# Expert weights in 4 MB transfers with rows of 32 KB into four double slots, in place of 2 MB transfers into eight slots

## What is computed

```
def expert_choice_ffn(h, w_router, w_gate, w_up, w_down):
    probs = softmax(einsum('bld,de->ble', h, w_router))     # 16 experts
    gate, idx = lax.top_k(transpose(probs, (0, 2, 1)), cap) # cap = 2 * 512 / 16 = 64 tokens an expert
    xs = h[idx]                                             # 16 x 64 x 1024
    a = einsum('becd,edf->becf', xs, w_gate)                # f = 2048
    u = einsum('becd,edf->becf', xs, w_up)
    y = einsum('becf,efd->becd', silu(a) * u, w_down)
    y = y * gate[..., None]
    return segment_sum(y, idx)                              # added back to the 512 tokens
```

## Time and profile before

| | us |
|---|---|
| median of 3 runs | 1852.03 (1851.35 to 1852.34) |
| the profiled execution | 1852.32 |
| its span in the trace | 1850.5 |
| TensorE matmuls busy in it | 1714.0 (93%) |
| weight loads of TensorE | 1045.3 |
| DVE busy | 658.1 |
| ACT busy | 447.3 |
| the queue of SP, share of 16 DMA engines | 66.0% |

### The profile page before, as it was taken

How to read it: one execution, slowest core, us unless ns; L and a number is a source line. 1 busy time by engine, 2 the same in 40 slices (tenths; PEclk the granted TensorE clock), 3 DMA queues, 4 the chain that set the end, 5 groups by cost and what they waited for, 6 DMA issues and landing times. The chain is left out here.

```text
span 1850.5 us, 20537 instructions
## 1 busy us (share of the span) xinstructions
PE 1714.0 (93%) x8653; PEld 1045.3 (56%) x8653; DVE 658.1 (36%) x916; ACT 447.3 (24%) x561; POOL 0.2 (0%) x4
## 2 busy tenths in 40 slices
PE   7999996999897997979979889799999999999998
PEld 6888873343332432324324243277778888888886
DVE  8985633001010110100101001057645565645745
ACT  5434331110000100101001010065333433423333
POOL 0000000000000000000000000000000000000000
PEclk9999998999999999999999999999999999999999
DMA  6235437999999999999999999970422223222311
GB/s 201 93 113 178 161 135 288 409 429 427 427 429 427 430 429 427 429 429 428 429 427 429 429 427 429 427 273 17 160 68 71 89 91 114 91 91 91 114 46 46
DMA packets 75050, 492.55 MB, mean 266 GB/s; under 512 B 7408, under 2 KB 11504, under 8 KB 49904
## 3 DMA queue, kind: packets, MB, share of 16 engines
q1 hardware_dynamic: 74992, 491.71, 66.0%
HBM read 487.49 MB, written 2.10 MB: 265 GB/s over the span
## 5 line engine op out<-in xcount | busy, mean ns | idle before, releaser
L1244 PE MATMUL ps<-xs,xe 128*64 128x512 f32 x2048 | 461.5, 598 | 67.2 <-DMA xs<-w_up 34.7
L1244 PEld LDWEIGHTS ps<-xs,xe 128*64 128x64 f32 x2048 | 141.8, 137 | 379.5 <-issue 264.5
L1256 PE MATMUL ps<-xs,hidT 128*64 128x512 f32 x960 | 215.0, 596 | 10.7 <-DMA xs<-w_down 6.6
L422 DVE TENSOR_TENSOR lo<-raw,hi 128x2048 fp32r<-128x2048 f32 x72 | 162.7, 2260 | 150.3 <-ACT hi L413 147.1
L1509 DVE TENSOR_TENSOR hid<-hid,ps 128x512 f32<-128x512 f32 x32 | 20.6, 684 | 525.8 <-PE ps L1244 525.8
L413 ACT ACTIVATE hi<-raw 128x2048 fp32r<-128x2048 f32 x72 | 136.1, 1890 | 185.0 <-PE ps L452 93.9
L476 PE MATMUL ps<-xh,hi 128*128 128x512 f32 x416 | 165.2, 397 | 2.3 <-issue 1.3
L476 PE MATMUL ps<-xl,hi 128*128 128x512 f32 x416 | 162.4, 390 | 0.0
L452 PE MATMUL ps<-xh,hi 128*128 128x512 f32 x384 | 150.2, 391 | 1.4 <-DVE xt L2088 1.1
L452 PE MATMUL ps<-xl,hi 128*128 128x512 f32 x384 | 149.5, 389 | 0.0
L1256 PEld LDWEIGHTS ps<-xs,hidT 128*64 128x64 f32 x960 | 68.8, 137 | 135.9 <-issue 112.7
(11 more groups left out here) (442 smaller groups left out, 1783.9 us busy)
## 6 DMA issues: line engine op xcount, KB each, us to landing
xs<-w_up SPq DMA_DIRECT2D x64, 2048.0 KB, 32.8
xs<-w_gate SPq DMA_DIRECT2D x64, 2048.0 KB, 32.0
xs<-w_down SPq DMA_DIRECT2D x60, 2048.0 KB, 31.1
raw<-w_in SPq DMA_DIRECT2D x24, 1024.0 KB, 7.8
raw<-ffn_up_w SPq DMA_DIRECT2D x24, 1024.0 KB, 5.1
raw<-ffn_down_w SPq DMA_DIRECT2D x12, 1024.0 KB, 5.0
raw<-w_out SPq DMA_DIRECT2D x8, 1024.0 KB, 5.1
xs<-w_down_q SPq DMA_DIRECT2D x2, 2048.0 KB, 36.7
```

The costliest lines, as they stand in the source:

```text
L422: dve.tensor_tensor(lo[slot][:, 0:size], raw[:, raw_slot(n), 0:size], hi[slot][:, 0:size].bitcast(F32), ALU.subtract).then_inc(sem("lo_don ...
L1244: mm = pe.matmul(ps[64 * half:64 * half + 64, bank + b, :], xe[:, k, CAP * u:CAP * (u + 1)], xs[n % NXS][:, f:f + 512], start=(k == 0), st ...
L1256: mm = pe.matmul(ps[64 * nn:64 * nn + 64, YB, :], hidT[:, 4 * (c % 2) + kk, CAP * half:CAP * (half + 1)], xs[n % NXS][:, kk * D + nn * 512 ...
```

## The change

Two chunks become one transfer of 4 MB. `expert_rows` gives 512 rows of w_gate or w_up, four to a partition, or 1024 rows of w_down, eight to a partition, 32 KB in one piece. Slots are four double tiles `xd`, and the old slots `xs` are halves of them, at places of their own. The first sixteen chunks are still issued as halves (`load_half`: 16 KB of each partition's 32 KB), each when the chunk eight before it is used; from chunk 16 on `load_x` issues a double transfer when both chunks of its slot are used. TensorE waits at even chunks only, for both halves or for the double transfer. The gather now takes every fourth column, the transposes every eighth, and they begin only when both halves of hid are made. The last four quarters stay as they are, with semaphores of their own (`q_sem`).

```diff
+NXD = NXS // 2
...
-    small[:, P_GX:NPRM] = i["norm2_g"][0].reshape(4, P, 2).transpose(1, 0, 2).reshape(P, KD)
+    small[:, P_GX:NPRM] = i["norm2_g"][0].reshape(2, P, 4).transpose(1, 0, 2).reshape(P, KD)
...
-        xs = [at(f"xs{j}", [P, XCH], F32, (0, 16, 32, 48, 102, 118, 64, 80)[j]) for j in range(NXS)]
+        xd = [at(f"xd{j}", [P, 2 * XCH], F32, (0, 32, 102, 64)[j]) for j in range(NXD)]
+        xs = [xd[j // 2][:, XCH * (j % 2):XCH * (j % 2) + XCH] for j in range(NXS)]
...
-        def expert_chunk(n, i=None):
-
-            e, j = divmod(n, 12)
+        def expert_rows(m, i=None):
+
+            e, j = divmod(m, 6)
             first = e if i is None else i * 2 + e
-            if j < 8:
-                return (wg, wu)[j // 4][bass.ds(first * D + 256 * (j % 4), 256), :].rearrange("(p k) n -> p (k n)", k=2)
-            return wd[bass.ds(first * FF + 512 * (j - 8), 512), :].rearrange("(p k) n -> p (k n)", k=4)
+            if j < 4:
+                return (wg, wu)[j // 2][bass.ds(first * D + 512 * (j % 2), 512), :].rearrange("(p k) n -> p k n", k=4)
+            return wd[bass.ds(first * FF + 1024 * (j - 4), 1024), :].rearrange("(p k) n -> p k n", k=8)
...
         def x_arrived(pe, n, i):
 
-            slot = n % NXS
-            before = 16 * in_first[2 * slot] if slot < 2 else 16 * (slot >= 5)
-            pe.wait_ge(x_sem(slot), i * (16 * 24 // NXS) + (before + 16 * (n // NXS + 1)))
+            base = 16 if n % NXS >= 6 else 0
+            if n % 2 == 0:
+                pe.wait_ge(x_sem(n), base + 32 if isinstance(i, int) and i == 0 and n < NXS else i * (16 * 24 // NXS) + (base + 48 + 16 * (n // NXS)))
...
         def gather(pe, k):
 
             o = ps[:, TB + k // 2 % 2, (k % 2) * P:(k % 2 + 1) * P]
-            d0 = 256 * (k // 2) + k % 2
+            d0 = 512 * (k // 4) + k % 4
             for t in range(NT):
-                mm = pe.matmul(o, htk[:, t, d0:d0 + 255:2], s1[:, t, :], start=(t == 0), stop=(t == NT - 1))
+                mm = pe.matmul(o, htk[:, t, d0:d0 + 509:4], s1[:, t, :], start=(t == 0), stop=(t == NT - 1))
...
+                    pe.wait_ge(sem("hid_done"), i * 4 + (2 * u + 2))
                     for b in range(2):
-                        pe.wait_ge(sem("hid_done"), i * 4 + (2 * u + b + 1))
                         for q in range(4):
-                            f = 512 * b + q
-                            mm = pe.transpose(ps[:, TB + b, q * P:(q + 1) * P], hid[:, f:f + 509:4], ident)
+                            f = 4 * b + q
+                            mm = pe.transpose(ps[:, TB + b, q * P:(q + 1) * P], hid[:, f:f + 1017:8], ident)
...
-            def load_x(n, i=None):
-
-                if i is not None:
-                    sp.wait_ge(sem("xs_used"), i * 24 + (n - NXS + 1))
-                elif n >= NXS:
+            def load_half(n):
+
+                if n >= NXS:
                     sp.wait_ge(sem("xs_used"), n - NXS + 1)
-                sp.dma_start(xs[n % NXS][:], expert_chunk(n, i)).then_inc(x_sem(n % NXS), 16)
+                rows = expert_rows(n // 2)
+                k = rows.shape[1] // 2
+                d(xs[n % NXS].rearrange("p (k n) -> p k n", k=k), rows[:, k * (n % 2):k * (n % 2) + k, :]) \
+                    .then_inc(x_sem(n), 16)
+
+            def load_x(m, i=0):
+
+                sp.wait_ge(sem("xs_used"), i * 24 + (2 * (m - NXD) + 2))
+                d(xd[m % NXD][:], expert_rows(m, i).rearrange("p k n -> p (k n)")).then_inc(x_sem(2 * m), 16)
...
-            for n in (2, 3, 6, 7):
-                load_x(n)
+            for n in (2, 3, 6, 7, *range(NXS, 2 * NXS)):
+                load_half(n)
             with sp.Fori(0, NE // 2 - 1) as i:
-                for n in range(NXS, NXS + 24):
-                    load_x(n, i)
-            for n in range(NX - 16, NX - 4):
-                load_x(n)
+                for m in range(2 * NXD, 2 * NXD + 12):
+                    load_x(m, i)
+            for m in range(NX // 2 - 4, NX // 2 - 2):
+                load_x(m)
```

More of the change, by code:

```diff
@@ L110, in lay_out @@
         "w_s": i["w_in"][0][:, 1024:1024 + SW].reshape(KD, P, SW).transpose(1, 0, 2),
-        "w_down_q": i["w_down"][0][NE - 1].reshape(4, P, 4, 4, 256).transpose(1, 3, 0, 2, 4).reshape(P, 4, XCH),
+        "w_down_q": i["w_down"][0][NE - 1].reshape(2, P, 2, 4, 4, 256).transpose(1, 4, 0, 2, 3, 5).reshape(P, 4, XCH),
         "gmlp_ws_t": i["gmlp_w_s"][0].transpose(2, 0, 1),
@@ L290, in build @@
         t1 = at("t1", [P, SEQ], F32, B + 49)
-        xs = [at(f"xs{j}", [P, XCH], F32, (0, 16, 32, 48, 102, 118, 64, 80)[j]) for j in range(NXS)]
+        xd = [at(f"xd{j}", [P, 2 * XCH], F32, (0, 32, 102, 64)[j]) for j in range(NXD)]
+        xs = [xd[j // 2][:, XCH * (j % 2):XCH * (j % 2) + XCH] for j in range(NXS)]
         x67 = at("x67", [P, 2, XCH], F32, 64)
         xq3 = at("xq3", [P, XCH], F32, B + 73)
-        last_home = (xs[4][:], xs[5][:], x67[:, :, XCH // 2:], xq3[:])
+        last_home = (xs[4], xs[5], x67[:, :, XCH // 2:], xq3[:])
         kr = at("kr", [P, RH, SEQ], F32, B)
@@ L359, in build @@
         in_first = [len(range(slot, NFIRST, 2)) if slot < 2 else 0 for slot in range(NRAW)]
-        LOADS_BEFORE = [in_first[slot] + (NX // NXS if slot % 2 == 0 else 0) for slot in range(NRAW)]
+        LOADS_BEFORE = in_first
         wg = w["w_gate"].rearrange("e d f -> (e d) f")
@@ L564, in build, with x_sem, q_sem, q_arrived @@
         GB, UB, YB, TB = 0, 2, 4, 5
-        def x_sem(slot):
-            return sem(f"raw_in{2 * slot}") if slot < 2 else sem(f"x_in{NXS - 1 - slot}")
+        def x_sem(n):
+            return sem(f"x_in{(3, 4, 5, 2)[n % NXS // 2]}")
         def x_arrived(pe, n, i):
-            slot = n % NXS
-            before = 16 * in_first[2 * slot] if slot < 2 else 16 * (slot >= 5)
-            pe.wait_ge(x_sem(slot), i * (16 * 24 // NXS) + (before + 16 * (n // NXS + 1)))
+            base = 16 if n % NXS >= 6 else 0
+            if n % 2 == 0:
+                pe.wait_ge(x_sem(n), base + 32 if isinstance(i, int) and i == 0 and n < NXS else i * (16 * 24 // NXS) + (base + 48 + 16 * (n // NXS)))
+        def q_sem(q):
+            return sem(f"x_in{(5, 0, 1, 2)[q]}")
+        def q_arrived(pe, q):
+            pe.wait_ge(q_sem(q), (16 * (NX // NXS + 2), 32, 32, 16 * (NX // NXS + 3))[q])
         def gather(pe, k):
             o = ps[:, TB + k // 2 % 2, (k % 2) * P:(k % 2 + 1) * P]
-            d0 = 256 * (k // 2) + k % 2
+            d0 = 512 * (k // 4) + k % 4
             for t in range(NT):
-                mm = pe.matmul(o, htk[:, t, d0:d0 + 255:2], s1[:, t, :], start=(t == 0), stop=(t == NT - 1))
+                mm = pe.matmul(o, htk[:, t, d0:d0 + 509:4], s1[:, t, :], start=(t == 0), stop=(t == NT - 1))
             if k % 2:
@@ L1305, in down_by_columns @@
                 for q in range(4):
-                    n = NX - 4 + q
-                    x_arrived(pe, n, 0)
+                    q_arrived(pe, q)
                     if q >= 2:
@@ L2280, in _ @@
             load_chunk(sp, 13)
-            def load_x(n, i=None):
-                if i is not None:
-                    sp.wait_ge(sem("xs_used"), i * 24 + (n - NXS + 1))
-                elif n >= NXS:
+            def load_half(n):
+                if n >= NXS:
                     sp.wait_ge(sem("xs_used"), n - NXS + 1)
-                sp.dma_start(xs[n % NXS][:], expert_chunk(n, i)).then_inc(x_sem(n % NXS), 16)
+                rows = expert_rows(n // 2)
[5 more added lines that the diff above has]
+                d(xd[m % NXD][:], expert_rows(m, i).rearrange("p k n -> p (k n)")).then_inc(x_sem(2 * m), 16)
             sp.wait_ge(sem("uz_done"), 4)
-            load_x(4)
-            load_x(5)
+            load_half(4)
+            load_half(5)
             load_chunk(sp, 14)
             sp.wait_ge(sem("glu_ps"), 1)
-            load_x(1)
+            load_half(1)
             for n in range(15, 19):
@@ L2303, in _ @@
             sp.wait_ge(sem("lo_done"), NFIRST)
-            load_x(0)
+            load_half(0)
             sp.wait_ge(sem("pe_used"), NFIRST)
-            for n in (2, 3, 6, 7):
-                load_x(n)
+            for n in (2, 3, 6, 7, *range(NXS, 2 * NXS)):
+                load_half(n)
             with sp.Fori(0, NE // 2 - 1) as i:
-                for n in range(NXS, NXS + 24):
-                    load_x(n, i)
-            for n in range(NX - 16, NX - 4):
-                load_x(n)
+                for m in range(2 * NXD, 2 * NXD + 12):
+                    load_x(m, i)
+            for m in range(NX // 2 - 4, NX // 2 - 2):
+                load_x(m)
             for q in range(4):
@@ L2316, in _ @@
                 src = w["w_down_q"][:, q, :]
-                d(last_home[q], src.rearrange("p (a b) -> p a b", a=2) if q == 2 else src).then_inc(x_sem(n % NXS), 16)
+                d(last_home[q], src.rearrange("p (a b) -> p a b", a=2) if q == 2 else src).then_inc(q_sem(q), 16)
             for j in range(4):
```

## The result

The changed kernel takes 1855.08 us (median of 16 runs, 1850.28 to 1856.14), the kernel before 1851.57 in the 16 runs beside it (1847.8 to 1854.12). The ratio is 1.0018, with a 95% interval of 1.0011 to 1.0024: slower by 3.3 us (2.0 to 4.4). The forecast was 1851.9 us and no change. The time lies in the range, but the kernel is slower clear of the noise, and the forecast had it stand still. The profiled execution has a span of 1853.6 us, against 1850.5.

A forecast was written before the change was run, and what follows sets the result against it. Weight transfers were taken to set the expert stage's pace, with TensorE slack except at its head and end. Rate -6.5, gather +1.2, head +1.0 and end +4.2 sum to -0.1 us: 1851.9 us, range 1847.5 to 1859.0.

The forecast's parts named there:

- The rate: Expert weight stream: 86 transfers of 4 MB each save 75 ns through longer rows, 6.5 us in all.
- the line: DMA row time per engine, fitted through 16 KB and 2 KB rows: 9.4 ns a row plus 36.8 ns a KB.
- (a): Weight stream: 32 KB rows cost as much per byte as 16 KB rows, no 6.5 us saving; 1858.3 us, chance 0.15.
- (b): Weight stream: long rows save only 2.4 us, a third of the row cost; 1856.0 us, chance 0.06.
- (c): Weight stream: all 75 ns above byte rate goes, saving 13.0 us; 1845.4 us, chance 0.14.
- The cover: Steady state of the stream: queued transfers outlast TensorE's late release of slots, 15 us left; costs nothing.
- The dry queue at the head: Head of the stream: transfer 8 waits for chunk 9 and starts into an empty queue; +1.0 us.
- The pair at the end: End of the stream: chunks 186 and 187 arrive together and both run after that arrival; +3.46 us.
- a gather record costs 19 ns more: First gather at the head, now stride 4: 64 slower records delay the release that starts chunk 12; +1.2 us.
- the transposes: End of the stream: stride 8 loads of 240 ns and waiting for both products of hid; +0.75 us.
- rival (d): TensorE's clock falls in longer waits for pairs; +1.7 us at the stream's end; anything past 3.7 us, chance 0.02.
- The second block: After 1226 us, where matmuls bound: the change touches none of it, so its length stays the same.

The follow-up runs named there:

- the probe: One profiled execution of the kernel before with other operands and strides in its gathers; no run time given; htk loads at stride 4: 330 ns as matmul, 208 as transpose.
- the first experiment: The changed kernel with htk written by ACT in the order the gather reads it; 1847.86 us, ratio 0.9985 to the kernel before.
- the version to keep: The changed kernel with htk in gather order, last pair in halves, and last expert's transposes at stride 4 with quarters to fit; 1846.32 us, ratio 0.9972.

## Why the prediction was right or wrong

**Right.** The rate: 6.5 us were forecast from the line through the rows' lengths; the window reads 431 GB/s, and the spans leave 6.3 to 6.5. The experiments with 16 KB rows in 4 MB and with 8 KB rows show that it is the row. Rivals (a), (b) and (c), and with them the ends of the range, are out by that. The Trainium skill's rule of about 3 bus cycles a packet (DMA: Bandwidth & Descriptors, Why small descriptors are slow) would have saved 2.4 us, an estimate; the runs do not agree with it. The cover: from 370 to 1190 us the share is 1.00 at 431 GB/s, and in windows of 5 us it is nowhere under 0.95. The dry queue at the head: 1.0 us forecast, 0.5 to 0.7 measured. The pair at the end: 3.46 forecast (a slip, (13.95 - 0.2) / 4 is 3.44), 3.44 in the timelines, and running the pair in halves brings 2.8 us back. Another slip cost nothing: the line's 36.8 ns a KB counts 1000 bytes a KB, and it is 37.7 for 1024.

**Wrong: the gather.** The step that failed is "a gather record costs 19 ns more", +1.2 us at the head. Its loads at stride 4 were priced by the row of the transposes at stride 4 (211 ns), an operation that the probe shows to be spared; a matmul's load takes 330. Its pitch went from 121 to (7.73 - 0.28) / 31 = 240 ns, 119 ns more for each of 64 records, 7.6 us if all were load-bound. At the head 5.1 us of it came through, since the first 32 records run largely at the lower clock (7.70 instead of 6.28 us) and the other two groups of 16 took 4.00 instead of 2.15 each; a shorter fall of the clock in chunks 4 to 7 (15.28 instead of 15.65 us) gave some of that back, which leaves the 4.6. The experiment with the stride alone puts +5.0 us into the trace of the kernel before. The bound that I gave, 2.4 us, did not hold it either: it was taken from the value and not from a second row. The gather was also the one place where TensorE's slack in steady state shrank, by 64 records x 119 ns = 7.6 us of 8.7 for two experts: the waits for transfers in the profile before, 72 us over the stage (34.7, 31.1 and 6.6), fell to 20. It cost nothing there, but only just.

**Wrong: the transposes.** 240 ns were extrapolated for stride 8; 193 were measured. Instead of 0.75 us the end pays 0.46.

**The clock, rival (d).** I gave it a chance of 0.02 because the one wait of 2.50 us in the trace was not followed by a fall. In the trace of the changed kernel the wait of 2.11 us before the last pair is, and it costs 1.7 us there. One wait without a fall was too little to go by; the mechanism was worth a larger chance. In the stage itself it is hidden by the stream.

**The second block and the noise.** That the second block would not change its length did not hold either: it is 1.7 us shorter, by the fall of the clock that only the kernel before has, and this hid half of the gather's error. Whether that is luck is open. And the forecast took 3.7 us for the least that a measurement can tell, which 16 runs beside 16 beat: they told 3.3 us with some 1.2 to either side.

By the sum: -0.1 as forecast, the gather +3.4 over its term, the clock at the end +1.7, the transposes -0.3, the rate and the dry queue together -0.3, the start 0.4 late, the second block -1.7: 3.1 us, by which the spans differ. The ratio of the runs gives 3.3.

## What to carry to other kernels

Price an operand's stride from a row of the same operation: a weight load with a stride of four float32 took 330 ns in a matmul and 208 to 211 in a transpose, against 190 to 192 without a stride. Where a transfer-bound stream starts on a release from TensorE, a delay ahead of that release is paid in full at the end of the stage (5.0 us at either place here), so layout work that a copy can do on the way (here ACT, at no cost that the runs show) belongs there. Larger transfers paid through longer rows, and what they took back stood at the two ends of the stream: keep those in small pieces, which was tried here at the end only.

## What was not expected of the hardware

The step of weight loads between strides of 2 and 4, nearly flat up to 8, and its absence in transposes, as above. And the granted clock fell more often where TensorE waited longer at a time. A window over the middle of the stage (PE busy, clock, DMA share, GB/s) of the first experiment, and a fall in the trace of the kernel before with htk laid out:

```profile
420.00:1150.00 730.00, 655.86 (x3002) 0.98 1.00 432
```
```profile
1174.91 8.78 PE L1244 MATMUL ps<-xs,xe 128*64 128x512 f32 x32 [2.04 <-DMA xs<-w_gate]
```

The kernel before has 1.00 in that window with nearly the same busy time (654.78 us), in waits of 1.24 us, none of which is followed by a fall. The pair-wise kernels with a fast gather wait 2.6 us at a time and show 0.98, in single falls to 0.50, of which a pair that takes 8.4 to 8.8 instead of 7.09 us is the mark. A long wait does not always bring one: of the eighteen waits of some 2.5 us or more for a pair in the first experiment eight are followed by a fall, of six over 2 us in the changed kernel two, and of the four over 1.9 us in the traces of kernels with single chunks one, the row above. In the changed kernel the slow gather takes up most of the waits, and the clock rounds to 1.00. Behind the head of the stage the falls cost nothing, since the stream bounds it; near its end each costs 1.7 us, also in the version to keep, whose first two quarters take 8.87 instead of 7.21 us. That the length of the waits causes them is argued from these counts and was not tried by itself.
